# Norms chunk by chunk, and the experts' down products in two column groups

## What is computed

```python
a = rmsnorm(h, norm_mix) * (1 + sc_m) + sh_m          # q = 0 in the kernel
u = a @ w_in
y = concat(ssd(u), hgrn2(u), gdn(u))                  # three scans, two directions each
h = h + g_m * (y @ w_out)
f = rmsnorm(h, norm_ffn) * (1 + sc_f) + sh_f          # q = 1 in the kernel
h = h + g_f * (routed_experts(f) + shared_expert(f))  # 64 experts, top 8 of them for each token
...
expert(x) = (silu(x @ w_gate) * (x @ w_up)) @ w_down  # 1024 -> 256 -> 1024
out = rmsnorm(h_latent, norm_final)                   # after the second layer
```

## Time and profile before

| what | number |
| --- | --- |
| median of 3 executions | 2814.97 us |
| the profiled execution: its own time, its span | 2812.39 us, 2810.7 us |
| granted TensorE clock, mean over the span | 0.948 |
| busy: TensorE, VectorE, ScalarE, GpSimd | 87%, 45%, 23%, 22% |
| first matmul of the input projection, layers 0 and 1 | 48.04 us, 1572.42 us |
| router's product begins, layers 0 and 1 | 766.93 us, 2139.31 us |
| experts' loop on TensorE, first gate and up to the end of the last down product, layer 0 | 841.0 to 1513.8 us |
| the same, layer 1 | 2180.9 to 2774.3 us |
| VectorE's additions and final norm at the end | 2790.93 to 2807.64 us |

### The profile page before, as it was taken

How to read it: one execution, slowest core, us unless ns; L and a number is a source line. 1 busy time by engine, 2 the same in 40 slices (tenths; PEclk the granted TensorE clock), 3 DMA queues, 4 the chain that set the end, 5 groups by cost and what they waited for, 6 DMA issues and landing times.

```text
span 2810.7 us, 45706 instructions
## 1 busy us (share of the span) xinstructions
PE 2448.0 (87%) x15116; PEld 1632.2 (58%) x15117; DVE 1266.5 (45%) x2832; ACT 643.9 (23%) x1146; POOL 610.6 (22%) x640
## 2 busy tenths in 40 slices
PE   5999888886789999999996798888877999999994
PEld 2347788885645555555553345787865555555552
DVE  4433487875333333333332553467853333333333
ACT  2116343231111111111110114523321111111111
POOL 0000354550002222222221000245320122222221
PEclk9999899997899999999998799999989999999998
DMA  6643100001539999999996251200017899999993
GB/s 259 244 175 76 19 2 1 1 1 35 195 136 319 367 352 349 344 343 341 364 336 192 99 201 60 49 1 1 1 43 276 314 365 374 376 354 361 364 367 115
DMA packets 187920, 574.26 MB, mean 204 GB/s; under 512 B 55742, under 2 KB 99078, under 8 KB 148870
## 3 DMA queue, kind: packets, MB, share of 16 engines
q1 hardware_dynamic: 162950, 520.48, 49.8%
q0 software_dynamic: 24832, 51.97, 8.0%
HBM read 554.89 MB, written 53.15 MB: 216 GB/s over the span
## 4 chain that ended last, share of the span: by engine, by line
PE 58%; DVE 15%; DMA 14%; issue 5%; ACT 4%; POOLq 2%; DVEq 2%; ACTq 1%; POOL 0%; SPq 0%
PE ps L1732 53%; DMA featT<-ffn_rows,idx_in 8%; PE ps L1736 5%; DVE R L1098 3%; DMA R<-ffn_rows,idx_in 3%; ACT R L832 2%; DVE featT L1098 2%; DVE ring L1098 1%; POOLq L744 1%; DVE R L1372 1%; DMA R<-in_exp_up 1%; ACT L832 1%; DVEq L1095 1%; DVE R L1101 1%; DMA R<-ffn_sum_even 1%
## 5 line engine op out<-in xcount | busy, mean ns | idle before, releaser
L1732 PE MATMUL ps<-R 128*64 128x256 f32 (+6 forms) x9040 | 1391.4, 379 | 68.9 <-DVEq L1377 19.3
L1732 PEld LDWEIGHTS ps<-R 128*64 128x64 f32 (+2 forms) x9040 | 850.1, 162 | 477.2 <-issue 250.5
L832 ACT ACTIVATE R<-ps 128x256 f32<-128x256 f32 (+3 forms) x395 | 175.5, 444 | 1047.7 <-PE ps L1732 993.7
L1098 DVE TENSOR_TENSOR R<-R,ps 128x256 f32<-128x256 f32 (+2 forms) x250 | 143.7, 575 | 439.8 <-ACT R L832 368.5
L1732 PE MATMUL ps<-featT,ring 128*128 128x512 f32 (+1 forms) x768 | 312.5, 563 | 0.3 <-issue 0.3
L1732 PE MATMUL ps<-ring,R 128*128 128x128 f32 (+2 forms) x1200 | 242.4, 334 | 16.3 <-DVE ring L1098 7.8
L1732 PEld LDWEIGHTS ps<-featT,ring 128*128 128x128 f32 x768 | 147.2, 196 | 161.8 <-issue 156.9
L1732 PEld LDWEIGHTS ps<-ring,R 128*128 128x128 f32 x1200 | 191.9, 196 | 49.1 <-issue 28.7
L1101 DVE TENSOR_SCALAR R<-ps,idx_out 128x512 f32<-128x512 f32 x128 | 96.1, 751 | 270.9 <-PE ps L1732 270.9
L1107 DVE COPY R<-ps 128x512 f32<-128x512 f32 (+2 forms) x280 | 153.8, 549 | 129.9 <-PE ps L1736 96.4
L669 POOL TENSOR_TENSOR R<-ring,lev 128x512 f32<-128x512 f32 x56 | 73.0, 1303 | 618.5 <-DVEq L1334 307.3
(11 more groups left out here) (201 smaller groups left out, 1974.3 us busy)
## 6 DMA issues: line engine op xcount, KB each, us to landing
R<-in_exp_gate SPq DMA_DIRECT2D x128, 1024.0 KB
R<-in_exp_up SPq DMA_DIRECT2D x128, 1024.0 KB
R<-in_exp_down SPq DMA_DIRECT2D x128, 1024.0 KB
R<-in_w_mod SPq DMA_DIRECT2D x48, 1024.0 KB, 7.4
ring<-in_w_in SPq DMA_DIRECT2D x30, 1024.0 KB, 5.3
ring<-in_w_out SPq DMA_DIRECT2D x8, 1024.0 KB, 8.0
ffn_sum_odd<-zero SPq DMA_DIRECT2D x6, 512.0 KB, 11.1
ffn_rows<-X SPq DMA_DIRECT2D x6, 512.0 KB, 5.4
```

What stands on the lines that cost most here:

```text
L832: do(C.activation(out_, in_, func, **kw), name)
L1098: do(V.tensor_tensor(out_, a, b, op), name)
L1732: return MM(out_, lhsT, rhs, start=start, stop=stop)
```

## The change

Three groups of edits are made. (1) The down product of an expert is done in units of 64 rows: the left half of the model's columns goes to column group 0 to 63 and the right half to 64 to 127 of the array; the second unit only if the expert has more than 64 tokens, for which TensorE's program reads `more` and branches once again in each step. The moves out of PSUM are two instructions of 64 partitions on each engine where they were one of 128. (2) Each norm goes chunk by chunk: sum, root (`Sqrt` on ScalarE, reciprocal on VectorE), scale and transpose of a chunk follow its last addition. ScalarE takes all eight pieces of a chunk, but for the last chunk, where VectorE takes four. The third and fourth blocks of `w_out` are multiplied chunk by chunk, so both have to be there first. (3) The tables are loaded in halves, the even one as soon as its scatters have landed, and the odd one's destination is `sums2`. The final norm is fused into one instruction, and `norm_final` is loaded early.

```diff
+            def xt_bank(q, c):
+                return bank((4, 0)[q] + 2 * (c % 2), 2)
+            def by_dve(c):
+                return KT // 2 if c == NT - 1 else 0
 @@ SyncE
-                wait("wo_sb", N_OUT, l)
+                wait("wo_sb", 2 + nl, l)
...
+                halves = ((live[:nl // 2], "sums_loaded"), (live[nl // 2:], "sums_b"))
+                wait("scattered0", 8 * NE, l)
+                for cs, name in halves:
+                    sp.dma_start(sums[:, rows, :], acc_dram.rearrange("(c p) f -> p c f", p=P)[:, rows]).then_inc(S[name], 16)
...
-                for b in range(2):
-                    wait(f"scattered{b}", 8 * NE, l)
-                sp.dma_start(yraw[:, rows, :], acc_odd.rearrange("(c p) f -> p c f", p=P)[:, rows]).then_inc(S["sums_loaded"], 16)
-                sp.dma_start(sums[:, rows, :], acc_dram.rearrange("(c p) f -> p c f", p=P)[:, rows]).then_inc(S["sums_loaded"], 16)
+                wait("scattered1", 8 * NE, l)
+                for cs, name in halves:
+                    sp.dma_start(sums2[:, rows, :], acc_odd.rearrange("(c p) f -> p c f", p=P)[:, rows]).then_inc(S[name], 16)
 @@ ScalarE
-                f(st[:, 4:8], st[:, 0:4], ACT.Ln, scale=1.0 / DM, bias=cst[:, 0:1])
-                f(st[:, 8:12], st[:, 4:8], ACT.Exp, "rstd", scale=-0.5)
+            def root(at_, l, c):
+                wait("sumsq", at_, l)
+                f(st[:, 4 + c:5 + c], st[:, c:c + 1], ACT.Sqrt, "rstd", scale=1.0 / DM, bias=cst[:, 0:1])
+                for n in range(2):
+                    root(at_ + n, l, live_[n])
+                if q == 0 and l == 0:
+                    mod_row(0)
+                for n, c in enumerate(live_):
+                    feats(q, n, c, l)
+                    if n + 2 < len(live_):
+                        root(at_ + n + 2, l, live_[n + 2])
...
-                    f(oe[s % 2][:, 0:512], ps[:, 4 + 2 * (s % 2), :], ACT.Identity, "oe_act", scale=idxS[s][:, 1:2])
+                    for u in range(2):
+                        at_ = slice(u * HD, (u + 1) * HD)
+                        ins = C.activation(oe[s % 2][at_, 0:512], ps[0:HD, 4 + 2 * (s % 2) + u, :], ACT.Identity, scale=idxS[s][at_, 1:2])
+                    do(ins, "oe_act")
 @@ VectorE
+            def norm_rows(q, l, n, c):
+                if n >= 2:
+                    wait("xT_ps", q * NT + n - 1, l)
+                sumsq(c)
+                inv_rms(q * (NT + 1) + n + 1, l, c)
+                ts(X[:, c % 2, :], h[:, c, :], st[:, 8 + c:9 + c], None, ALU.mult, name="xn")
...
+                    head(0)
+                    for c in range(2):
+                        norm_rows(0, 0, c, c)
                     mod_add(0)
+                    for c in range(2, NT):
+                        norm_rows(0, 0, c, c)
+                    turned(0, NT - 1, NT - 1, 0)
...
+                for n, c in enumerate(live):
+                    wait("wo_ps", 2 + n + 1, l)
+                    tt(sqo[:, 0, 0:2 * BW], ps[:, 4 + c, :], grow[:, c // 2, 2 * BW:DM], ALU.mult)
+                    tt(h[:, c, 2 * BW:DM], h[:, c, 2 * BW:DM], sqo[:, 0, 0:2 * BW], ALU.add, "wo_sb")
+                    norm_rows(1, l, n, c)
...
-                    ts(oe[s % 2][:, 512:DM], ps[:, 5 + 2 * (s % 2), :], idxS[s][:, 1:2], None, ALU.mult, name="oe_dve")
+                    for u in range(2):
+                        at_ = slice(u * HD, (u + 1) * HD)
+                        ins = V.tensor_scalar(oe[s % 2][at_, 512:DM], ps[HD:P, 4 + 2 * (s % 2) + u, :], idxS[s][at_, 1:2], None, ALU.mult)
+                    do(ins, "oe_dve")
...
+                    tt(sums[:, c, :], sums[:, c, :], sums2[:, c, :], ALU.add)
                     tt(sums[:, c, :], sums[:, c, :], bank(2 * (c // 2), 2), ALU.mult)
                     tt(h[:, c, :], h[:, c, :], sums[:, c, :], ALU.add)
+                    if l + 1 < DEPTH:
+                        norm_rows(0, l + 1, n, c)
+                    else:
+                        sumsq(c)
+                        inv_rms(NT + 1 + len(live) + n + 1, l, c)
+                        stt(X[:, c % 2, :], h[:, c, :], st[:, 8 + c:9 + c], fin, ALU.mult, ALU.mult, "out_ready")
 @@ TensorE
+                        if k == KT - 1:
+                            for c in range(2):
+                                norm_turn(0, 0, c, c)
                         mod_mm(k, whd[k])
...
+                for n in (2, 3):
+                    ring_wait(N_IN + n, l)
+                for x, c in enumerate(live):
+                    for n in (2, 3):
+                        for k in range(KT):
+                            ins = mm(ps[:, 4 + c, (n - 2) * BW:(n - 1) * BW], yT[:, k, tk(c)], ring[:, (N_IN + n) % 2, k, :], k == 0, k == KT - 1)
+                    ins.then_inc(S["wo_ps"], 1)
+                    if x == nl - 1:
+                        pe.drain().then_inc(S["ring_used"], 2)
+                    if x:
+                        norm_turn(1, l, x - 1, live[x - 1])
+                norm_turn(1, l, nl - 1, live[-1])
...
+                def down_rows(s, u):
+                    for k in range(2):
+                        for half in range(2):
+                            ins = mm(ps[half * HD:(half + 1) * HD, 4 + 2 * (s % 2) + u, :], hTe[s % 2][:, k, u * HD:(u + 1) * HD],
+                                     wdn[s][:, k, half * 512:(half + 1) * 512], k == 0, k == 1)
...
+                    pe.sem_inc(S["past"], 1)
+                    wide = pe.value_load(more[0:1, slice(j, j + 1) if isinstance(i, int) else bass.ds(j, 1)], min_val=0, max_val=1)
+                    with pe.If(wide > 0):
+                        down_rows(s, 0)
+                        down_rows(s, 1).then_inc(S["dn_ps"], 1)
+                    with pe.Else():
+                        down_rows(s, 0).then_inc(S["dn_ps"], 1)
```

More of the change, by code:

```diff
@@ L1078, in _ @@
                     act.sem_inc(S["ov_sl"], OVER)
-            wait("sumsq", 1, DEPTH)
-            f(st[:, 4:6], st[:, 0:2], ACT.Ln, scale=1.0 / DM, bias=cst[:, 0:1])
-            f(st[:, 8:10], st[:, 4:6], ACT.Exp, "rstd", scale=-0.5)
+            for n, c in enumerate(LIVE[DEPTH - 1]):
+                root(NT + 1 + len(LIVE[DEPTH - 1]) + n + 1, DEPTH - 1, c)
         @block.vector
@@ L1151, in mod_add, with sumsq @@
                 dve.drain().then_inc(S["mod_sb"], 1)
[L1153 to L1169 removed]
+            def sumsq(c):
+                V.tensor_tensor_reduce(out=X[:, c % 2, :], in0=h[:, c, :], in1=h[:, c, :], scale=1.0, scalar=0.0,
+                                       op0=ALU.mult, op1=ALU.add, accum_out=st[:, c:c + 1])
+                dve.drain().then_inc(S["sumsq"], 1)
@@ new lines, in inv_rms, with head @@
+            def inv_rms(at_, l, c):
+                wait("rstd", at_, l)
+                do(V.reciprocal(st[:, 8 + c:9 + c], st[:, 4 + c:5 + c]))
+            def norm_rows(q, l, n, c):
[4 more added lines that the diff above has]
+                ts(X[:, c % 2, :], h[:, c, :], st[:, 8 + c:9 + c], None, ALU.mult, name="xn")
+            def head(l):
+                wait("prm_ps", 1, l)
+                cp(prm[:, :], ps[:, 7, 0:N_PRM], "prm_sb")
+                cp(lowv[:, 0, :], low[:, l:l + 1, :].rearrange("p o t -> p (o t)"))
+                ts(lowv[:, 2, :], lowv[:, 0, :], -1.0, 1.0, ALU.mult, ALU.add)
+                ts(lowv[:, 1, :], lowv[:, 0, :], 1e-30, float(2.0 ** 40), ALU.max, ALU.mult, "low_c")
@@ L1534, in _ @@
                     cp(nrow[:, base + 2 * HD:base + 4 * HD], nrow[:, base:base + 2 * HD])
-                wait("rstd", 2, l)
+                wait("rstd", NT + 1, l)
+                yq = slice(live[0], NT)
+                do(V.reciprocal(ssq[:, yq, :], ssq[:, yq, :]))
                 for c in live:
```

162 lines of the change are left out of this document (66 added, 96 removed).

## The result

The kernel after took 2823.09 us (median of 20 executions, 2813.80 to 2831.44), the kernel before 2814.23 us (20, on the same chip). The ratio is 1.0036, 95% interval 1.0026 to 1.0046: slightly slower, by 9 us. I had said 2785 us with 0.82 for faster, and a range that ended at 2812. So sign and range were both missed. The profiled execution after is of 2818.49 us (span 2816.4); the one before was of 2812.39.

What follows compares the result with a forecast made beforehand. TensorE (95% busy in the experts' loops) was taken to bind, with DMA and gathers close behind. Against the profiled 2812.4 us: +3.5 - 4 - 15 - 9.5 + 9 - 15 - 5 + 6 = -30, 2782; median 2785, range 2757 to 2812.

Steps and rivals of the forecast that it cites:

- The step on the output projection: Layer 0, last blocks to router: shorter tail -13.4 us against later blocks, transposes and cold clock; sum -4 (-8 to +1).
- The floor by bytes: Layer 1's experts' loop: weights trickle in until about 2755 us, so the loop can shorten by 15 us at most.
- Rival 2: Experts' loops give nothing, as the DMA engines have no share left; 2815 us, no change; chance 0.10.
- The gathers' loop: Experts' loops: gathers set the pace of two narrow steps, 18.1 us becoming 17.6, a gain of 0.5.
- the second moves: Moves out of PSUM in every experts' step: +0.75 us before GpSimd's scatter and gather (0.4 to 0.8).
- The shorter products: Narrow experts' down products in two column groups: 1.8 us instead of 3.5, saving 1.7 in 94 narrow steps.
- The branch: TensorE's added read and branch before each down product: about 1.0 us, of which 0.4 exposed (0 to 1.0).
- The clock: Experts' loops: TensorE falls to half clock after long waits, 3 more times per layer; +6 us (0 to +40).
- Rival 3: Slower: waits collect into one gap, the clock falls at every second narrow pair or more; 18 falls give 2826 us; chance 0.10.
- head: Start of the kernel: first product of layer 0 moves from 48.04 to 51.5 us; +3.5 (-2 to +6).
- between the layers: From layer 0's experts to layer 1's first product: half tables land earlier, norm by chunks; -9.5 us (-14 to -4).
- layer 1's start: Start of layer 1's experts: their weights are issued later, after the last block is added; +9 us (+4 to +11).

Runs made afterwards that it cites:

- norms_only: Kernel after with the whole down products and single moves of the kernel before; 2828.29 us, ratio to before 1.0052.
- norms_apart: Kernel after without column groups, gathers in the old order, FFN rows' stores and `sh_down` on ScalarE's queue; 2800.26 us, ratio to before 0.9956.
- gather_early: Kernel after with GpSimd gathering rows four pairs ahead before it scatters its own pair's sums; 2813.97 us, ratio to before 1.0009.
- apart_early: Kernel after with gathers ahead of scatters, FFN rows' stores and `sh_down` on ScalarE's queue; 2792.39 us, ratio to before 0.9939.
- down_only: Kernel before with the down products in column groups, their branch and moves, and nothing else; 2811.71 us, ratio to before 0.9997.
- less_after: Kernel after with 2 MB instead of 3 MB loaded per layer 1 expert after the first four (other output); 2795.95 us, layer 1's loop 560.8 us.
- before_moves: Kernel before with each move of the down product's sums split in two of 64 rows on VectorE and ScalarE; 2853.73 us, ratio to before 1.0142.
- both_units: Kernel after without TensorE's branch, both units of 64 rows always multiplied, two moves kept; 2880.79 us, ratio to before 1.0240.
- less_early: Kernel after with gathers ahead of scatters and 2 MB instead of 3 MB per layer 1 expert after the first four; 2701.23 us, layer 1's loop 473.3 us.
- less_before: Kernel before with 2 MB instead of 3 MB loaded per layer 1 expert after the first four (other output); 2793.74 us, layer 1's loop 574.7 us.
- apart_early_nogroups: Kernel after with early gathers, FFN rows' stores and `sh_down` on ScalarE's queue, and down products as before; 2791.75 us, ratio to before 0.9928.

## Why the prediction was wrong

**The term that was missing: the stores in layer 0, +15.3 us.** The step on the output projection counted to the router and stopped. It did not follow SyncE's queue past the point where the experts' loads start. Shown: norms_only has the delay, norms_apart has not, and the difference of their ratios (1.0052 and 0.9956) is 27 us for both layers. By the sums it is also what made the sign wrong: 2823 less 15 is 6 us below before. The kernel after with only this mended was not run; with early gathers in both, the same move (gather_early to apart_early) took the ratio from 1.0009 to 0.9939.

**The floor by bytes was mis-sized, and stood in one layer only.** The prediction put it 15 us below layer 1's loop, from the time when the last weights trickle in the earlier trace rows, and named none for layer 0. The reading of that row was wrong: in the trace of the kernel before, packets of 4096 bytes of the weights' queue still come until 2765.5 us, not 2755, the last of them one after another every 0.16 us. The last down product takes 3.7 us behind them, so the room below the loop's end at 2774.3 was some 5 us and not 15. Six kernels with early gathers measured it: their loops take 662 to 670 us in layer 0 and 588 to 594 in layer 1, with column groups or without, with one move or two. That is 3 to 11 us below the kernel before in layer 0 and 0 to 5 in layer 1. (The kernel after itself reached 585.8 in layer 1, which is within what I can read.) By the Trainium skill, "DMA: Bandwidth & Descriptors", "Specifications", about 358 GB/s, the 206 MB of layer 1's loop would take an estimated 575 us, 18 less than it took before; so my sentence that by this figure the loops could not be shortened at all was wrong. In the stretches above the trace has 367 GB/s, and the loop has its first and last experts besides, when the DMA engines have little to fetch (34 GB/s from 2760 to 2764 us before). I had used the stretch of 373 GB/s to set the figure aside; it was right enough to say that the loops could not get much shorter. Rival 2 (0.10, the experts give nothing) was nearest to the true case (down_only: 0.9997), and I should have weighed, both shares near 1, more than the trickle.

**The gathers' loop was right in size, and its gain stayed unseen.** 17.3 us measured for narrow pairs in less_after, where bytes do not hide it, against 17.6 predicted. The gain of 0.5 for each circuit was not measured: the same pairs took 18.1 us on average before and 18.2 after. Of its two parts, the second moves were priced well: 0.75 in 32 circuits is 24 us for a loop, and before_moves lost 20.5 in each. The shorter products were sized too high: 15 and 17 us of gain with these 24 put back are 39 and 41 us, and both_units lost 27 and 34.

**The products were right.** At the full clock eight instructions took 1.94 us (1.8 predicted), and two moves 1.52 on VectorE (1.5). The branch exposed less than the 0.4 predicted: from the start of the transposes to the start of the down product it was 0.93 us before and 1.02 after at the median, and 0.18 more on average.

**The clock was under-sized, and the loops did not show it.** Over the 400 us of layer 1 shown above the granted clock was 0.93, not 0.95 or more; before it was 0.99. TensorE's busy time for the same instructions in layer 1's loop was 499.3 us in the kernel after and 467.8 in less_early, where the clock was 1.00, so about 31 us went to it; in the kernel before it was 8 (562.3 and, in less_before, 554.1). The clock's term is thus some 23 us of TensorE's time in this loop, where I had 3. In gather_early it did not come back, it moved: the down products took 134.0 us instead of 148.6 and the transposes into gathered rows 51.3 instead of 60.0, but gate and up took 279.0 instead of 255.6, because the waits now stand before them. Whether it cost anything: apart_early and apart_early_nogroups ran layer 1's loop at 0.93 and 0.98 and took 593.7 and 593.6 us. So where the gathers are early it cost nothing that the bytes did not already cost; for the kernel after itself no run separates the two. Rival 3 is no explanation of the slower time, as both loops were no longer than before.

**The other norms' terms** were right within 2 us: head +3.4 (+3.5), output projection -4.0 (-4), between the layers -7.7 (-9.5), end -4.3 (-5), layer 1's start +11.0 (+9). For the output projection the parts agree too: the fourth block's products ended at 758.34 instead of 745.52, of which 3.4 is the head, so 9.4 later (9.5 to 11.5), and the tail behind them took 8.0 us (8). In layer 1 `sh_down` was waited for again, kernel after, beside the earlier trace rows:

```profile
2124.12 15.88 PE ps L1775 x64
...
2166.14 18.60 DMA ring<-in_sh_down
```

**Open.** How much of the 0.5 and 7.5 us that the two loops gained is scatter, and how much of the 27 us between norms_only and norms_apart belongs to `sh_down` and how much to the stores; they were moved together.

## What to carry to other kernels

Where two engines both show a share near 1.0 in a stretch, take work away from the other one in an experiment (here: bytes) before you pay for taking it from the first; here TensorE's saving came through in full only when both the bytes and the gathers had gone. When a step is moved, follow each queue that it issues to, down to the next small transfer behind it: 12 MB issued 11 us later cost 15 us at stores of 0.5 MB that had not moved at all. And read the end of a loop from the last packet that it needs, not from where the engines' share falls. And count an added instruction by the loop that it stands in, not by its engine's busy share: 0.75 us on an engine that was 38% busy (and 0.7 on ScalarE beside it) cost 40 us in all.

## What the runs showed of the hardware

Small stores issued by ScalarE while SyncE's queue had megabytes of loads under way landed in 7.5 us, where on SyncE's queue behind those loads they took 20.6 (medians of six stores in both layers). And a move of 64 rows by 512 columns takes as long as one of 128 rows, 755 and 751 ns on VectorE, 681 and 689 ns on ScalarE, so halving rows saves nothing. And the last weights of a stream of 1 MB loads came in late: in the kernel before the DMA engines' rate fell to 104 GB/s in 2748 to 2752 us, and the last packets came at 2765.5.
